# Two steps' scores side by side, squares added before they are summed, and more idle products around the choice of experts

## The reference, cut to what matters

```
proj = h @ w_in[layer]
o_dil = _dilated_attention(...)            # 8 heads
o_fox = _forgetting_attention(...)         # 8 heads
o_dil = _rmsnorm(o_dil.reshape(B, T, D_DIL), out_norm_dil[layer])
o_fox = _rmsnorm(o_fox.reshape(B, T, D_FOX), out_norm_fox[layer])
x = x + jnp.concatenate([o_dil, o_fox], axis=-1) @ w_out[layer]
h2 = _rmsnorm(x, ffn_norm[layer]).reshape(B * T, D)
y = _hierarchical_moe(h2, ...)             # top group, then top-2 of its 8 experts
```

## Time and profile before

| | us |
|---|---|
| median of the runs | 1351.03 |
| lowest and highest of three runs | 1348.68, 1352.02 |
| the profiled execution, as timed | 1345.8 |
| its span in the profile | 1343.9 |
| PE busy | 1282.6 (95%) |
| DVE, ACT, POOL busy | 661.0, 526.1, 534.1 |
| mean granted clock of TensorE | 0.98 |

### The profile page before, as it was taken

The page is one execution under the profiler, slowest core; times in us unless marked ns, Lnnn a source line. Parts: engine busy times, 40 slices in busy tenths (PEclk is TensorE's granted clock), DMA queues, the critical chain, the costliest instruction groups (busy, mean ns, idle before and its releaser), DMA issues. The chain is left out here.

```text
span 1343.9 us, 20487 instructions
## 1 busy us (share of the span) xinstructions
PE 1282.6 (95%) x7796; PEld 927.8 (69%) x7796; DVE 661.0 (49%) x1356; ACT 526.1 (39%) x1121; POOL 534.1 (40%) x548
## 2 busy tenths in 40 slices
PE   7999999999999999999999999999999989999995
PEld 6766777878888877677889987667668833333332
DVE  5456994157741579864774431544444511111125
ACT  4312333356742434435664333755452221111111
POOL 0214698344445446974345412754251111111121
PEclk9999999999999999999999999999989699999998
DMA  9772111130012321021002231311046769999985
GB/s 391 301 294 96 46 47 48 51 153 1 2 64 96 115 79 63 37 98 55 1 2 71 77 100 62 117 64 57 23 157 271 302 249 416 420 421 415 417 348 208
DMA packets 42512, 209.57 MB, mean 156 GB/s; under 512 B 7255, under 2 KB 9687, under 8 KB 33184
## 3 DMA queue, kind: packets, MB, share of 16 engines
q1 hardware_dynamic: 34192, 194.59, 37.1%
q0 software_dynamic: 5760, 10.27, 2.0%
q10 hardware_dynamic: 2448, 3.21, 0.8%
HBM read 201.46 MB, written 17.30 MB: 163 GB/s over the span
## 5 line engine op out<-in xcount | busy, mean ns | idle before, releaser
L438 POOL TENSOR_TENSOR wlo<-raw,whi 128x512 fp32r<-128x512 f32 x102 | 141.3, 1389 | 141.0 <-ACT whi L426 136.0
L3413 PE MATMUL ps<-gu,XT 128*64 128x512 f32 x608 | 138.0, 601 | 8.0 <-DVE XT L3521 5.1
L426 ACT ACTIVATE whi<-raw 128x512 fp32r<-128x512 f32 x124 | 76.8, 629 | 147.7 <-PE ps L881 110.7
L1165 DVE SCALAR_TENSOR_TENSOR z<-glu,small,z 128x798 f32<-128x798 f32 (+1 forms) x120 | 132.6, 1154 | 0.8
L881 PE MATMUL ps<-hxh,whi 128*128 128x512 f32 x304 | 128.7, 424 | 0.6 <-ACT whi L426 0.5
L881 PE MATMUL ps<-hxh,wlo 128*128 128x512 f32 x304 | 119.9, 394 | 2.1 <-POOL wlo L438 2.1
L881 PE MATMUL ps<-hxl,whi 128*128 128x512 f32 x304 | 120.1, 395 | 0.0
L3413 PEld LDWEIGHTS ps<-gu,XT 128*64 128x64 f32 x608 | 45.5, 138 | 87.9 <-issue 77.4
L1708 POOL TENSOR_SCALAR P<-P,stat 128x768 f32<-128x768 f32 (+1 forms) x80 | 65.5, 821 | 72.3 <-DVE stat L1670 71.4
L1617 ACT ACTIVATE P<-ps,stat 128x768 f32<-128x768 f32 (+1 forms) x80 | 65.2, 815 | 59.0 <-DVE stat L1663 58.3
L1663 DVE TENSOR_REDUCE stat<-ps 128x1 f32<-128x768 f32 (+1 forms) x72 | 66.7, 926 | 22.5 <-PE ps L1568 22.1
(11 more groups left out here) (847 smaller groups left out, 3190.8 us busy)
## 6 DMA issues: line engine op xcount, KB each, us to landing
gu<-in_w_gu_dram SPq DMA_DIRECT2D x32, 2048.0 KB, 16.4
raw<-in_w_in_dram SPq DMA_DIRECT2D x66, 512.0 KB, 3.3
dn<-in_w_dn_dram SPq DMA_DIRECT2D x32, 1024.0 KB, 16.6
wgate<-in_w_mod_dram SPq DMA_DIRECT2D x16, 1024.0 KB, 8.0
raw<-in_w_out_dram SPq DMA_DIRECT2D x24, 512.0 KB, 3.3
wmod<-in_w_mod_dram SPq DMA_DIRECT2D x4, 2048.0 KB, 14.9
ybuf<-zero SPq DMA_DIRECT2D x1, 4096.0 KB, 12.5
yin<-ybuf SPq DMA_DIRECT2D x4, 1024.0 KB, 8.2
```

What stands on the lines that cost most here:

```text
L426: e.activation(K.hi[i][:, half(h)], K.raw[i % 2][:, half(h)], ACT.Copy).then_inc(*q.up("hi", i, h))
L438: e.tensor_tensor(K.lo[i][:, half(h)], K.raw[i % 2][:, half(h)], K.hi[i][:, half(h)].bitcast(F32), ALU.subtract).then_inc(*q.up("lo", i, h))
L1165: e.scalar_tensor_tensor(o, x, weight, o, ALU.mult, ALU.add).then_inc(*q.up("conv", l, i, j))
L3413: m = e.matmul(s[o, :], x[:, k, o], gu[:, k, :], start=k == 0, stop=k == KT - 1, skip_group_check=True)
```

## The change

The scores of two steps now stand together: in each even step g the walk writes those of g + 2 and of g + 3, and in odd steps none. The squares of four pairs are added before PE sums them: each pair's squares keep their own buffer (`square_of`), POOL adds pair 1 to pair 0 and pair 2 to that at i = 1 (one addition of 128x512 each), DVE adds pair 3 behind its `y2l`, and PE runs the four products with ones once for a half, so twice instead of eight times; the place in PSUM that was held for the sums over a half is held no more. In the choice, four idle products stand right behind the router's last product and one behind each of twelve steps (before: five steps); in the placing one stands behind each of eleven steps and four behind `here` (before: six in all). The sixteen behind the lists are now issued at the start of the experts' part, behind the end of the stage `chosen`, so that other engines' waits for that stage end with the second list.

```diff
 def square_of(p):
-    return 3 if p < 2 else (p - 2) % 4
+    return (p + 3) % 4
@@ second_walk
-        if later + 1 < len(UNITS) // 2:
-            scores(later + 1)
+        if g % 2 == 0:
+            for ready in (later + 1, later + 2):
+                if ready < len(UNITS) // 2:
+                    scores(ready)
         finish()
@@ PE
     def weigh_sums(p):
-        if p % 4 == 0:
-            held["norm", p // 4] = K.bk.hold("mean", "y2", p // 4)
-        s, before = held["norm", p // 4]
-        sums_pe(S, s, before, C.tmp[square_of(p)], ("ssq", "y2", p), T2, [("y2sq", p)], p % 4 == 0, p % 4 == 3)
         if p % 4 == 3:
-            K.bk.release("mean", "y2", p // 4)
+            s, before = K.bk.take("mean", "y2", p // 4)
+            sums_pe(S, s, before, C.tmp[square_of(p)], ("ssq", "y2", p), T2, [("y2sums", p)])
@@ DVE, weigh_lo
+        if p % 4 == 3:
+            a, b = (C.tmp[square_of(j)][:, :] for j in (p, p - 1))
+            for w in q(("y2sq", p), ("y2sums", p - 1)):
+                e.wait_ge(*w)
+            e.tensor_tensor(a, a, b, ALU.add).then_inc(*q.up("y2sums", p))
@@ POOL, weigh_sums
+        if p % 4 in (1, 2):
+            a, b = (C.tmp[square_of(j)][:, :] for j in (p, p - 1))
+            for w in q(("y2sq", p), ("y2sq", p - 1) if p % 4 == 1 else ("y2sums", p - 1)):
+                e.wait_ge(*w)
+            e.tensor_tensor(a, a, b, ALU.add).then_inc(*q.up("y2sums", p))
@@ PE, place
-        for step in ("key4", "other4", "key1", "M1", "key2"):
+        for _ in range(4):
+            keep_warm("logitsmm", 3)
+        for step in ("max", "e4_max", "key4", "k1", "other4", "v1", "key1", "k2", "M1", "v2", "key2", "k3"):
             keep_warm("choose", 3, step)
...
-        for step in ("cmp", "inc", "H2", "MM", "whole", "here"):
+        for step in ("cmp", "nb", "inc", "past", "H2", "G3", "p16b", "MM", "slot", "whole", "hi"):
             keep_warm("place", step)
+        for _ in range(4):
+            keep_warm("place", "here")
...
-        for i in range(WARM):
-            m = keep_warm("listmm")
-        m.then_inc(*q.up("warm"))
+        K.warm = lambda: keep_warm("listmm")
@@ experts_pe, ahead of experts_walk
+    for i in range(WARM):
+        m = K.warm()
+    m.then_inc(*q.up("warm"))
+    K.bk.release("warm")
```

More of the change, by code:

```diff
@@ L2392, in weigh @@
         e.activation(C.y[p // 4][0][:, p % 4, :], s[:, :], ACT.Copy, scale=K.small2[:, 8 + p:9 + p]).then_inc(*q.up("y2h", p))
-        for w in q(*((after("start3"), [("ssq", "y2", 0)], [("fC", 3)], [("fC", 3)], [("fC", 3), ("forget_rest",)])[p] if p < 5 else [("ssq", "y2", p - 4)])):
+        for w in q(*((after("start3"), [("fC", 3)], [("fC", 3)], [("fC", 3), ("forget_rest",)], [("y2sums", 1)])[p] if p < 5 else [("y2sums", p - 3) if p < 7 else ("ssq", "y2", 3)])):
             e.wait_ge(*w)
@@ L2747, in place @@
                 m.then_inc(*q.up("listmm"))
-        for i in range(WARM):
-            m = keep_warm("listmm")
-        m.then_inc(*q.up("warm"))
+        K.warm = lambda: keep_warm("listmm")
         K.bk.places.append((s, (("place", "H1"), ("place", "many"))))
-        K.bk.release("warm")
     last_walk(S, out=lambda t, c: out2_pe(S, 1, t, c), turn=turn, logits=logits, place=place)
```

## The result

| | before | after |
|---|---|---|
| median, us (11 runs each) | 1351.03 | 1354.28 |
| lowest and highest, us | 1345.02, 1353.43 | 1351.28, 1363.36 |
| the profiled execution, us (its span) | 1345.8 (1343.9) | 1360.25 (1358.4) |

What follows compares the result with a forecast made beforehand. PE's queue was taken to bound the kernel, with half-clock stretches. Second block 0, clock +3.9 and choice to experts -6.2 gave -2.3 us against the median 1351.0: 1348.7, range for 8 in 10 from 1342.5 to 1355.5.

Steps and rivals of the forecast that it cites:

- The clock at the new waits: Second block: five new PE waits bring 2.5 falls to half clock, costing 3.9 us, bounds 0 and 8.
- The tail behind step 24: Second block's end: pairing still saves 0.3 us per pair, sums 0.91 each; step 25's 1.70 us wait grows by 0.6.
- The waits for `y2l`: Second block: PE idles 2.75 us in steps 5, 9, 13 and 2.1 in 17, 21; 12.5 us, old waits' 2.5 off.
- The sums: Second block: six of eight sums on PE go, saving 5.5 us; additions on POOL and DVE cost nothing.
- Pairing: Second block: scores of two steps together save 0.3 us for each of 15 pairs, 4.5 us, bounds 1.5 and 6.
- The choice: Choice, lists and experts' start: clock stays at 1.00, lists shorten, second gather's wait goes; 6.2 us gained, bounds 3 and 8.4.
- the new wait for the first gather: Experts' start: transpositions may wait idle for the gather, losing the clock to the first up products; 0.6 us set against the gain.
- The rival in which narrow products don't hold the clock: Choice: narrow products do not lift the clock, only some 2 to 3 us gained, about 1352 us; chance 0.13.
- The rival in which nothing falls: Second block: five waits leave the clock at 1.00 and pairing saves its upper bound; 1341 to 1345 us, chance 0.25.
- The rival that came in: Second block: each new wait takes the clock with it in all five steps; +4.5 to +9 us, 1355.5 to 1360, chance 0.14.
- The carry to the end: From the second up products on: what PE gains before the next weight load, the loads gain too, one to one.

Runs made afterwards that it cites:

- The unpaired kernel: The changed kernel with the scores of one step in each step again, sums and idle products kept; 1338.38 us, ratio 0.9929 against the kernel before.
- the one without waits: The changed kernel with DVE making `y2l` ahead of the maxima of both steps; 1336.07 us, ratio 0.9905 against the kernel before.
- timing the part alone: The kernel before with only the choice's and placing's new idle products and the warm products' late end; 1344.30 us, ratio 0.9971.

## Why the prediction was wrong

The direction was wrong: -2.3 us forecast, +7.8 measured (5.1 to 10.4). The traces say +10.8 in the second block (three with the changed one, four with the old one) and -5.0 from there to the third up products, +5.8 in all. The five pairs give 10.1 of the 10.8: 13.7 for the new waits and 7.1 for the clock, less 2.0 for the old waits, 3.6 for four sums and 5.1 for the pairing. By its own steps:

**The clock at the new waits: the term that failed.** I took 2.5 falls at 1.58 us, 3.9 in all. In the five pairs, the waits by themselves make 94.6 + 3 x 2.83 + 2 x 2.61 = 108.3 us. The three traces took 117.0, 115.9 and 113.3: the clock cost 8.7, 7.6 and 5.0, on average 7.1. There were 4, 4 and 3 falls in five waits. That is 3.7 falls at 1.9 us, and both numbers were too low. The 1.58 from the one fall in the earlier trace rows, where up products went from 7.09 to 8.67, was right for the slow stretches of 3.4 us, eight of the eleven. The other three were 6.8 us long and cost 2.7 or 2.8. Too few falls make 1.9 us of the error and the long ones 1.3: mis-sized by 3.2 us, the largest error of the sum. One place of the same trace was not used, where the clock fell for 6.8 us behind a wait of only 1.41 us in the tail (PE's timeline, and the window behind it):

```profile
983.20 0.89 PE L2274 MATMUL ps<-ident,P 128*128 128x128 f32 x4 [1.41 <-POOL P L2523]
```

```profile
984.00:991.00 7.00, 6.62 (x24) 5.12 (x24) 3.75 (x12) 3.65 (x9) 3.65 (x4) 0.51 0.48 153
```

It shows the longer kind of fall, and that a wait need not be over 2 us for one. The prediction's reading, that the clock outlives a single 1.70 us, was true of that row and not of the kernel: in all six traces with unpaired scores a wait of 1.41 to 1.44 us at this place was followed by half clock within some 2 us. Two or three other waits of 0.5 to 1.7 us stand in the 12 us ahead of it, and whether these share in it was not tested.

**The tail behind step 24: mis-sized by about 3.** I gave the pairing 0.3 us there for each of three groups and the sums 0.91 twice, and only 0.6 for the longer wait in step 25: 2.1 us less than before. The three traces have 84.1 us from there to the router's end, the four old ones 83.4: 0.7 more. The unpaired kernel has 80.8, so the sums did their part (1.8 us forecast) and the pairing cost some 3. A part of these is clock, since the unpaired trace has 3.4 us at half clock there and the three have 6.8 to 10.2. The rest is waits: the one in step 29 went to 2.33, in step 25 to 2.61 from 1.70, and ACT's copy kept the weighing waiting by 0.78. My sum had the wait for `y2l` in six steps only and left step 29 out, where 0.38 stood before. With `y2l` first, ending the pairs at step 24 took 2.4 us off this part in the trace (81.1 against 83.5), which the timing could not confirm.

**The waits for `y2l`: right in three steps, 0.5 us short in two.** 2.75 forecast in steps 5, 9 and 13, measured 2.84, 2.83, 2.84. In steps 17 and 21 2.1 forecast, measured 2.61: the fourth product stands in the even step's scores too, so it delays PE by 0.4 us (a group of 1.89 instead of 1.49) and DVE's start by half of that, where I took 0.6 and nothing. That is 1.0 us for both. The old waits in the five steps were 0.27, 0.49, 0.49, 0.47 and 0.26, so 2.0 and not the 2.5 that I took off.

**The sums: right.** 0.91 each, four in the five pairs. The additions were hidden there, as said. **Pairing: above its upper bound in the five pairs, and nothing elsewhere.** 1.25 us for a dilated pair of heads between the unpaired kernel (19.7) and the one without waits (18.45), of which 0.27 was the old wait; so 0.5 for each group of two steps, where 0.3 was taken and 6 us for fifteen was the upper bound, 0.4; 2 us more than forecast in the five pairs. Ahead of them (steps 0 to 3) the kernels with pairs and those without both take 19.8 to 19.9 us, so two groups saved nothing, and behind step 24 the pairing cost time, as said.

**The choice: the mechanism right, the sum 1.2 too high.** 6.2 forecast; 5.0 between the means of the traces, 3.9 (1.1 to 6.7) by timing the part alone. The clock stayed at 1.00, the lists took 1.98 and 1.99 us where 1.85 and 1.9 were forecast, the first transposition was 4.6 earlier between the two first traces and 3.6 between the means of all (5.1 forecast), the sixteen idle products took 3.84 us where 3.4 was forecast, and the second gather was no longer waited for. The weak step was the new wait for the first gather: 0.6 us was set aside for a lost clock there, and in three of six traces it cost 1.4 to 2.9. The rival in which narrow products don't hold the clock fell for this mixture with idle products; narrow products alone were not tried.

**The rivals.** The rival in which nothing falls needed waits that leave the clock alone. The rule of the Trainium skill (TensorE: Matmul & The Clock Gate, the section on HAM oscillation), by which idle gaps of this size wouldn't bring the gate down, does not agree with the trace: eleven of fifteen waits of 2.6 to 2.8 us were followed by a fall. The warning of the Trainium skill in the same page's section on a second HAM failure mode, that short idle spells between groups of products can make the clock go up and down, is nearer to what was seen, though here one idle spell of 2.6 to 2.8 us in some 23 us was enough. The rival that came in was the last, that each new wait takes the clock with it, though only 11 of 15 did; idle products at half clock ahead of the lists did not happen. Its +4.5 to +9 us held the measured 7.8 in part by luck, since the loss in the tail was not in it. It was given 0.14, too little, since its main condition was the step that I knew least about. That the median of 1354.28 lies inside the forecast's range of 1342.5 to 1355.5 is no merit: a gain was forecast and a loss came.

The carry to the end held. In the changed kernel, the difference to before is 13.1 us at the third up products and the same until a slow stretch at 1203. Behind it the difference is 15.3, and 14.5 at the end, so no more than 0.8 was given back.

## What to carry to other kernels

When two groups of work are put together on one engine, look at what the next engine has queued behind the first group: here an instruction of 0.74 us that frees a place in PSUM went behind 1.5 us of maxima, and moving that one instruction ahead turned a loss of 0.6% into a gain of 1%. A new idle time of TensorE has two prices, its own length and that of the clock behind it, so size the second from every slow stretch that a trace shows, not from one row. And compare traces stage by stage: where the same code differs by 7 us from run to run, the spans say little about a change of 8.

## What the hardware showed that was not expected

- Whether an idle time costs TensorE's clock depends on more than its length: in the five pairs waits of 1.15 to 1.37 us never did (five waits), 2.6 to 2.8 did in 11 of 15 cases, and in the tail of the block 1.41 to 1.44 us, with two or three other waits of 0.5 to 1.7 in the 12 us before, did in six of six. In the same kernel the same wait was followed by no slow stretch, one of 3.4 us or one of 6.8 us in different pairs and runs. Slow stretches of 3.4 us cost 1.5 to 1.7 us, those of 6.8 us 2.7 or 2.8, in work bound by PE: somewhat less than half their length, since part of a stretch can lie in the wait itself.
- Router products of 36 and list products of 39 and 78 columns, with idle products of 128 columns between the steps, ran at a granted clock of 1.00 throughout (20 us) in six of eight traces; in the other two 3.4 us at the start were at 0.50, and neither was the slower for it (44.1 and 44.3 us to the third up products). With idle products at fewer steps 20.5 to 23.9 us of the same stage were at 0.50 in all five traces.
- Code that is the same and runs first reached the second block between 838.9 and 846.4 us in thirteen executions, with 10 to 24 us of it at half clock.
- What decides between no fall, a short and a long one behind the same wait was not tested and stays open.
